# Running sums of the log decays of gated linear attention: one-pass fp32r products of a high and a low part in place of full fp32 products

## The reference

```python
la = log_sigmoid(ra @ w_alpha_up + b_alpha) / 16      # 256 tokens x 512, for each direction
cum = jnp.cumsum(la, axis=3)                          # within chunks of 64 tokens
last = cum[:, :, :, -1:, :]
q_dec = q * jnp.exp(cum)
k_intra = k * jnp.exp(-cum)
k_state = k * jnp.exp(last - cum)
```

## Time and profile before

| what | us |
|---|---|
| median of 3 runs | 2012.54 |
| lowest, highest | 2009.66, 2013.27 |
| the profiled execution | 2011.93 |
| its span in the trace | 2010.1 |
| PE busy | 1916.9 (95%) |
| DVE busy | 1242.8 (62%) |
| ACT busy | 998.0 (50%) |

### The profile page before, as it was taken

How to read it: one execution, slowest core, us unless ns; L and a number is a source line. 1 busy time by engine, 2 the same in 40 slices (tenths; PEclk the granted TensorE clock), 3 DMA queues, 4 the chain that set the end, 5 groups by cost and what they waited for, 6 DMA issues and landing times.

```text
span 2010.1 us, 24905 instructions
## 1 busy us (share of the span) xinstructions
PE 1916.9 (95%) x9121; PEld 1563.6 (78%) x9121; DVE 1242.8 (62%) x2041; ACT 998.0 (50%) x1510; POOL 127.9 (6%) x52
## 2 busy tenths in 40 slices
PE   7999999999999999999999999999799999999996
PEld 6777888888777888877777787888677778878885
DVE  6756673547756674557569566575566684666645
ACT  4445554444445554444634745454546356464544
POOL 0000018200000008300000000000000000000000
PEclk9999999999999999999999999999989999999998
DMA  6444555556444555555534344656444343455562
GB/s 221 136 136 116 177 179 178 181 184 187 132 122 124 178 179 177 186 172 144 188 121 126 126 155 154 194 157 209 142 120 146 111 146 126 157 157 183 174 199 73
DMA packets 167499, 315.32 MB, mean 157 GB/s; under 512 B 12282, under 2 KB 20172, under 8 KB 167252
## 3 DMA queue, kind: packets, MB, share of 16 engines
q1 hardware_dynamic: 166784, 312.01, 50.1%
q10 hardware_dynamic: 596, 1.73, 0.2%
HBM read 312.65 MB, written 1.05 MB: 156 GB/s over the span
## 4 chain that ended last, share of the span: by engine, by line
PE 88%; DVE 6%; ACT 4%; issue 2%; DMA 0%; ACTq 0%; DVEq 0%
PE acc L542 76%; PE mix L514 4%; PE mix L582 2%; DVE lo L1279 1%; PE mix L786 1%; ACT hi L960 1%; PE mix L757 1%; ACT junk L1004 1%; PE mix L551 1%; DVE x L1362 1%; PE mix L776 1%; PE mix L570 0%; PE mix L744 0%; DVE kT L1297 0%; PE mix L716 0%
## 5 line engine op out<-in xcount | busy, mean ns | idle before, releaser
L960 ACT ACTIVATE hi<-raw 128x1024 fp32r<-128x1024 f32 x600 | 634.5, 1061 | 636.5 <-PE acc L542 591.7
L1279 DVE TENSOR_TENSOR lo<-raw,hi 128x1024 fp32r<-128x1024 f32 x552 | 666.2, 1226 | 242.6 <-ACT hi L960 227.2
L542 PE MATMUL acc<-hi,xTh 128*128 128x512 f32 (+3 forms) x1760 | 699.9, 398 | 15.1 <-DVE lo L1279 6.3
L542 PE MATMUL acc<-lo,xTh 128*128 128x512 f32 (+3 forms) x1760 | 684.0, 389 | 0.0
L542 PE MATMUL acc<-hi,xTl 128*128 128x512 f32 (+3 forms) x1760 | 684.0, 389 | 0.0
L542 PEld LDWEIGHTS acc<-hi,xTh 128*128 128x128 f32 x1760 | 338.4, 192 | 92.5 <-issue 25.5
L542 PEld LDWEIGHTS acc<-hi,xTl 128*128 128x128 f32 x1760 | 337.7, 192 | 67.7
L542 PEld LDWEIGHTS acc<-lo,xTh 128*128 128x128 f32 x1760 | 338.8, 192 | 61.3
L542 PE MATMUL acc<-hi,hTh 128*128 128x512 f32 x432 | 171.8, 398 | 0.3 <-DVE lo L1279 0.3
L933 POOL TENSOR_TENSOR lo<-raw,hi 128x1024 fp32r<-128x1024 f32 x48 | 127.7, 2687 | 693.7 <-ACT hi L960 693.7
L542 PE MATMUL acc<-hi,hTl 128*128 128x512 f32 x432 | 171.2, 396 | 0.0
(11 more groups left out here) (212 smaller groups left out, 1620.9 us busy)
## 6 DMA issues: line engine op xcount, KB each, us to landing
raw<-in_w_in SPq DMA_DIRECT2D x200, 512.0 KB, 3.8
raw<-in_w_ffn_in SPq DMA_DIRECT2D x80, 512.0 KB, 4.3
raw<-in_w_mlp_up SPq DMA_DIRECT2D x64, 512.0 KB, 3.9
raw<-in_w_mlp_down SPq DMA_DIRECT2D x64, 512.0 KB, 4.6
raw<-in_w_ffn_out SPq DMA_DIRECT2D x44, 512.0 KB, 4.3
raw<-in_w_out SPq DMA_DIRECT2D x32, 512.0 KB, 4.2
raw<-in_w_o_gla SPq DMA_DIRECT2D x16, 512.0 KB, 3.8
raw<-in_w_o_attn SPq DMA_DIRECT2D x16, 512.0 KB, 3.7
```

The source lines that it names most:

```text
L542: last = nc.tensor.matmul(out, a[:, t * P:(t + 1) * P], w[:, slot, part, 0:c.n], start=(k == 0 and a is ah and w is L.hi), stop=(k == c.k_ ...
L960: nc.scalar.activation(L.hi[:, slot], L.raw[:, slot], ACT.Copy).then_inc(*n.up("hi_ready"))
L1279: v.tensor_tensor(L.lo[:, slot], L.raw[:, slot], L.hi[:, slot].bitcast(F32), ALU.subtract).then_inc(*n.up("low_by_dve"))
```

## The change

ACT now copies the four constant matrices once per layer into `sums`, an fp32r tile (`sums_ready`). For each direction ACT copies the decays into an fp32r tile, the high part (`decays_high`), and DVE subtracts that from the decays, which gives the low part (`decays_split`). Each of the four products of a direction becomes two fp32r passes over the same bank, constant times high part and constant times low part. The chunk totals (L716 before) still read the fp32 decays and stay full fp32. The new tiles lie in memory that is free at the time: the high parts on `soft`.

```diff
--- before.py
+++ after.py
@@ -173,6 +173,9 @@
 
 
 SIGNALS = {
+    'sums_ready'          : [2, 0, 0],
+    'decays_split'        : [4, 0, 0],
+    'decays_high'         : [4, 0, 0],
     'unit_used'           : [600, 0, 0],
     'hi_ready'            : [600, 0, 0],
     'raw0_loaded'         : [150, 0, 0],
@@ -409,6 +412,8 @@
         states = at("states", 16, [P, 2, 3, GLA_V])
         raT = at("raT", 16, [P, NT, P])
         ra_rows = at("ra_rows", 17, [P, NT, P])
+        sums = at("sums", 18, [P, 4, P], F32R)
+        decay = [[at(f"decay{i}{d}", 4 * d + 8 * (i == "l"), [P, NT, COLS], F32R) for d in range(2)] for i in "hl"]
         qd = at("qd", 22, [P, NT, COLS])
         kd = at("kd", 26, [P, NT, COLS])
         seenT = at("seenT", 22, [P, 2, 2, NT, P])
@@ -453,7 +458,7 @@
         L.qT, L.qd, L.raT, L.raw, L.seenT, L.sems, L.small = qT, qd, raT, raw, seenT, sems, small
         L.soft, L.states, L.tmp, L.vm, L.wide, L.x, L.y = soft, states, tmp, vm, wide, x, y
         L.junk, L.gain_rows, L.gain_cols, L.embed, L.ple_gate, L.stationary = junk, gain_rows, gain_cols, embed, ple_gate, stationary
-        L.ra_rows = ra_rows
+        L.ra_rows, L.sums, L.decay = ra_rows, sums, decay
         block = ctx.enter_context(nc.Block())
 
         @block.tensor
@@ -705,11 +710,13 @@
         s.on(4)
         for d in range(2):
 
-            pe.wait_ge(*n.next("decays_ready"))
-            for t in range(NT):
-                for what in ("cum", "rest"):
-                    fill(("gla", what, d, t), lambda b: [nc.tensor.matmul(L.mix[:, b, :], L.cst(f"{what}_{'fb'[d]}"),
-                                                                         L.y[:, t, d * COLS:(d + 1) * COLS], **f32)])
+            if d == 0:
+                pe.wait_ge(*n.next("sums_ready"))
+            pe.wait_ge(*n.next("decays_split"))
+            for t in range(NT):
+                for i, what in ((d, "cum"), (2 + d, "rest")):
+                    fill(("gla", what, d, t), lambda b: [nc.tensor.matmul(L.mix[:, b, :], L.sums[:, i, :], L.decay[part][d][:, t, :],
+                                                                         start=(part == 0), stop=(part == 1)) for part in range(2)])
             def chunk_sums(b):
                 for h in range(GLA_H):
                     for t in range(NT):
@@ -1148,10 +1155,16 @@
             act.wait_ge(*n.next("magnitude", NT))
             nc.scalar.activation(L.soft[:, d], L.soft[:, d], ACT.Exp, scale=-1.0).then_inc(*n.up("logarithm"))
             s.on(1)
+        act.wait_ge(L.sems["const_loaded"], 32)
+        at = CONST_AT["cum_f"][0]
+        nc.scalar.activation(L.sums[:, :, :], L.const[:, at:at + 4 * P].rearrange("p (i c) -> p i c", i=4), ACT.Copy).then_inc(*n.up("sums_ready"))
         for d in range(2):
             act.wait_ge(*n.next("logarithm"))
             nc.scalar.activation(L.soft[:, d], L.soft[:, d], ACT.Ln, bias=1.0).then_inc(*n.up("softplus"))
-            s.on(1)
+            s.on(d)
+            act.wait_ge(*n.next("decays_ready"))
+            nc.scalar.activation(L.decay[0][d][:, :, :], L.y[:, :, d * COLS:(d + 1) * COLS], ACT.Copy).then_inc(*n.up("decays_high"))
+            s.on(1 - d)
         for d in range(2):
             for t in range(NT):
                 b = filled(("gla", "cum", d, t))
@@ -1741,6 +1754,8 @@
             link(v.tensor_tensor(la, la, L.soft[:, d], ALU.subtract), "decays_ready")
             if d == 0:
                 s.on(1)
+            dve.wait_ge(*n.next("decays_high"))
+            v.tensor_tensor(L.decay[1][d][:, :, :], la, L.decay[0][d][:, :, :].bitcast(F32), ALU.subtract).then_inc(*n.up("decays_split"))
         for d in range(2):
 
             b, use = L.banks.get((ln, "gla", "last", d))
```

## The result

The changed kernel takes 2027.05 us, the median of 4 runs (2024.35 to 2030.11), against 2012.33 for the kernel before, the median of 4. The ratio is 1.0075, 95% interval 1.0059 to 1.0091: slower by about 15 us. The profiled execution took 2024.49, with a span of 2022.7, 12.6 more than before. The four runs fall in two groups, near 2024.4 and near 2029.9, so no run lies near the median.

A forecast was written before the change was run, and what follows sets the result against it. It took ACT, not PE, as the bound ahead of the first direction's L716. Chain 11.2, clock 3.0 and products 0 gave 14.2 us on 2011.93, so 2026.1, and 2026.7 as median; range 2021.5 to 2031.5.

The forecast's parts named there:

- The products hidden: Products in all four places: PE's 6.5 us saving never reaches the end, as L716 waits for ACT's `kd`; taken as 0.
- the -0.3 that I had as a bound: Lower bound on the products' effect, should ACT start its first Exp sooner; the forecast itself took 0.
- the rival of fp32r passes that are no faster: Products still take 3.45 us, leaving the time unchanged; it shares the forecast's number, with no separate chance.
- The chain of the first direction: Constants' copy and ACT-DVE-ACT round trips delay L716 in each layer's first direction: +5.60 us each, 11.2 together.
- The wait behind the products: First direction: PE idles 2.8 us after the products, waiting for `kd`; the listed sign said 2 to 3 us.
- The sign of 13.2 us from the Ln table load to the totals: First direction: stretch from last Ln table load to L716 grows by 5.6 us, from 7.6 to 13.2.
- The clock: PE's clock falls in the two places that kept the upper level: 2 x 1.5 = 3.0 us, bounds 0 and 6.
- the sign that the clock would be below 1 behind all four: Profile after: granted clock below 1 behind L716 in both directions of both GLA layers.
- the rival with longer falls: Each lower-clock stretch in the four places lasts twice as long: 11.2 + 6, 2030 and above; chance 15%.

## Why the prediction was right, and where it was short

Forecast 2026.7, measured 2027.05; slower, as said. That the two agree to 0.4 us is luck: the median lies in the middle between two groups of runs 5.5 us apart. For the profiled execution the sum gave 2026.1, and it took 2024.49.

- **The products hidden.** Right. In the second direction, where nothing else was altered, the totals start 3.62 us behind the first product in both layers (3.92 in the first before, 3.62 in the second); that is the -0.3 that I had as a bound. With the high part alone it was 3.63, and with the passes made twice 3.67. But that the work is hidden does not make it free to take away: the rival of fp32r passes that are no faster was to have "the forecast's number", and the two kernels with full or double passes were 6 us shorter than the changed one.
- **The chain of the first direction.** Forecast +5.60 per layer, measured 5.70 and 5.69. Each step stands in the chain as worked out. The copies placed later show that 3.3 us of it are the order in which ACT and DVE meet; what is left, 2.4, is about the three copies' own time on ACT (0.50 and two of about 1.0). The high part alone moved the totals by the one step that was its own.
- **Signs that failed.** The wait behind the products was forecast at 2.8 us (2 to 3 among the signs) and is 0.92 and 0.82, since the sum had the passes at full clock behind a stop of 5.1 us. The sign of 13.2 us from the Ln table load to the totals was wrong by its own working: the constants' copy stands ahead of that load, so its 0.50 is not in the stretch, which measured 12.82.
- **The clock.** The size was right by two errors. I took two new falls at 1.5 us, in the first layer's two directions. In the shorter profile there were +1.47 in the first layer's first direction and +1.57 in the second layer's second, where the low stretch became longer than before rather than new; in the longer one the first layer's second direction lost 3.07 more. So the sign that the clock would be below 1 behind all four held in three of four places of the first profile (it was 1.00 behind the first layer's second direction). The term is 3.0 us in the profile of one group of runs and about 6 in that of the other; the rival with longer falls, which had 15%, is what the longer group does. I had put the falls down to the standing still ahead of the totals. For the second direction the passes made twice bear this out, as far as standing still and smaller work can be told apart. For the first it is not shown: filling the waits did not hold the clock.
- **The Trainium skill's rule** ("TensorE: Matmul & The Clock Gate", section "Why this matters for your kernels") that long idle gaps between bursts cost the clock spoke against the change. The trace agrees for the products of the first direction: the clock was 0.54 behind the stop of 5.12 us, and 1.00 where the stop was filled. Counted on the long stops alone the rule would have spared the second direction; there the trace of the longer group disagrees, since 1.6 us of idle followed by the two-column matmuls cost 3.1 us.
- **Left open.** What decides in a single execution whether the clock falls in the first layer's second direction, why the copies placed later gave three runs above 2030 and one at 2021.94, and why the clock falls behind the first direction's totals with the waits filled, was not separated.

## What to carry to other kernels

Before making the work of an engine at 95% cheaper, look at what the next instruction behind that work waits for: here it was an exponential on ACT, so the saving became idle time, and in the second direction that idle time ahead of a few tiny matmuls cost PE its clock. Put the work that does not need the contested buffer first: this order alone gave about 5 us. With it, and with one engine making both halves of the split off the chain of waits, the same cheaper products are worth something, though here only in the second direction.

## What the runs showed of the hardware

- More matmuls can make it shorter: 16 extra fp32r matmuls of 512 columns took the median from 2028.24 to 2022.53.
- A low stretch does not end as soon as PE is busy again. In the kernel with the copies behind both Ln the granted clock was 0.58 over the 14 us from 984 to 998, with PE busy all of it; the weight matmuls started at 990.45 and stood 0.43 us apart until 995.7.
- At the lower clock an fp32r matmul of 512 columns costs 0.43 us between starts (983.80 and 984.23 in the changed kernel's trace) against 0.23 at the upper.
- DVE's cast of 128 x 1024 to fp32r took 0.70 us, the subtraction of that size 1.22, ACT's copy 1.06.
